# Chunked scan of a hybrid block: cumulative steps made once and broadcast by DMA, decays formed on ScalarE, two products moved to GpSimd

## The reference

```
xdt = x * dt[..., None]
a_cum = jnp.cumsum(dt * a.reshape(G, R), axis=2)
seg = a_cum[:, :, :, None] - a_cum[:, :, None]
decay_ls = jnp.exp(jnp.where(causal, seg, -jnp.inf))
cb = jnp.einsum("bclgn,bcsgn->bclsg", cm, bm)
y_diag = jnp.einsum("bclsg,bclsgr,bcsgrp->bclgrp", cb, decay_ls, xdt)
decay_to_end = jnp.exp(a_cum[:, :, -1:] - a_cum)
states = jnp.einsum("bclgn,bclgr,bclgrp->bcgrpn", bm, decay_to_end, xdt)
...  # h <- h * exp(a_cum[-1]) + states, from chunk to chunk
y_off = jnp.einsum("bclgn,bcgrpn,bclgr->bclgrp", cm, h_start, jnp.exp(a_cum))
y = y_diag + y_off + x * d_skip.astype(f32).reshape(G, R)[:, :, None]
```

## Time and profile before

| | us |
|---|---|
| median of three runs | 2776.07 |
| profiled execution | 2777.77 |
| its span | 2776.1 |
| TensorE busy (matmul) | 2617.1 |
| VectorE busy | 1783.4 |
| GpSimd busy | 1590.2 |
| ScalarE busy | 1307.3 |

### The profile page before, as it was taken

How to read it: one execution, slowest core, us unless ns; L and a number is a source line. 1 busy time by engine, 2 the same in 40 slices (tenths; PEclk the granted TensorE clock), 3 DMA queues, 4 the chain that set the end, 5 groups by cost and what they waited for, 6 DMA issues and landing times. The chain is left out here.

```text
span 2776.1 us, 41535 instructions
## 1 busy us (share of the span) xinstructions
PE 2617.1 (94%) x14314; PEld 1845.0 (66%) x14314; DVE 1783.4 (64%) x2181; ACT 1307.3 (47%) x2067; POOL 1590.2 (57%) x1222
## 2 busy tenths in 40 slices
PE   4799999997999999899989999999999999599998
PEld 3588777776888888666655555555555555478887
DVE  4632356536313545189979888898988989555554
ACT  2433333344333333211148787877877778422221
POOL 3777666678777777468746666566655666000000
PEclk8799999998999999999989999999999999799999
DMA  2343333332433333335551212212122111333231
GB/s 103 99 145 135 105 120 106 125 102 89 160 118 109 127 133 118 102 82 134 131 169 33 86 61 62 77 39 85 62 62 68 48 39 58 112 127 106 76 107 44
DMA packets 202405, 267.97 MB, mean 97 GB/s; under 512 B 12832, under 2 KB 136032, under 8 KB 195568
## 3 DMA queue, kind: packets, MB, share of 16 engines
q1 hardware_dynamic: 202224, 265.64, 30.1%
HBM read 168.84 MB, written 96.76 MB: 96 GB/s over the span
## 5 line engine op out<-in xcount | busy, mean ns | idle before, releaser
L1935 POOL TENSOR_TENSOR a_w<-a_beta,a_rest 128x1024 f32<-128x1024 f32 (+2 forms) x320 | 560.8, 1753 | 354.6 <-DVE a_rest L1892 208.1
L808 POOL TENSOR_TENSOR f_l_lo<-f_wst,f_l_hi 128x512 fp32r<-128x512 f32 x312 | 407.2, 1308 | 273.6 <-ACT f_l_hi L702 272.6
L1892 DVE TENSOR_TENSOR_SCAN a_rest<-a_keep,a_rest,a_ones 128x513 f32<-128x513 f32 x384 | 469.9, 1261 | 10.8 <-ACT a_keep L1862 10.8
L1812 PE MATMUL a_turn<-a_ident,a_w 128*128 128x128 f32 (+1 forms) x2432 | 343.7, 279 | 7.3 <-DVE a_wt L1846 6.1
L1827 PE MATMUL a_o<-a_wt,a_v 128*64 128x512 f32 (+3 forms) x1408 | 339.6, 561 | 8.9 <-DVE a_out L1902 8.9
L1846 ACT COPY a_wt<-a_turn 128x512 f32<-128x512 f32 (+3 forms) x440 | 225.3, 528 | 208.0 <-PE a_turn L1812 206.5
L1812 PEld LDWEIGHTS a_turn<-a_ident,a_w 128*128 128x128 f32 (+1 forms) x2432 | 257.4, 140 | 91.5 <-issue 65.4
L1862 ACT ACTIVATE a_keep<-a_z 128x1024 f32<-128x1024 f32 (+4 forms) x352 | 299.8, 852 | 4.5 <-PE a_z L1795 4.5
L702 ACT ACTIVATE f_l_hi<-f_wst 128x512 fp32r<-128x512 f32 x312 | 195.7, 628 | 222.2 <-PE f_y L605 106.6
L1862 ACT ACTIVATE a_beta<-a_z 128x1024 f32<-128x1024 f32 (+4 forms) x352 | 299.6, 851 | 0.0
L605 PE MATMUL f_y<-f_t_hi,f_l_hi 128*128 128x512 f32 x624 | 249.9, 401 | 14.8 <-DVE f_u L1093 9.3
(11 more groups left out here) (228 smaller groups left out, 4988.6 us busy)
## 6 DMA issues: line engine op xcount, KB each, us to landing
f_wst<-in_w_pairs SPq DMA_DIRECT2D x52, 1024.0 KB, 5.4
scratch_gate<-f_out SPq DMA_DIRECT2D x64, 256.0 KB, 2.2
o_g<-scratch_mixed SPq DMA_DIRECT2D x32, 512.0 KB, 5.6
s_xc<-scratch_xbc SPq DMA_DIRECT2D x16, 768.0 KB, 5.2
scratch_xbc<-f_out SPq DMA_DIRECT2D x36, 256.0 KB, 2.1
scratch_q_hi<-f_out SPq DMA_DIRECT2D x32, 256.0 KB, 3.3
scratch_q_lo<-f_out SPq DMA_DIRECT2D x32, 256.0 KB, 3.6
scratch_v<-f_out SPq DMA_DIRECT2D x32, 256.0 KB, 2.3
```

Source lines behind the costliest of these rows:

```text
L808: return nc.gpsimd.tensor_tensor(out, a, b, op).then_inc(done, 1)
L1812: mm = nc.tensor.transpose(turn[h][0:rows, qi * P:(qi + 1) * P], tile[:, h, x:x + rows], ident[:, :])
L1892: mm = nc.vector.tensor_tensor_scan(rest[r % RS][:, h, tn - 1::-1], top, ones[:, 0:1].to_broadcast([P, tn]), start, ALU.mult, ALU.min)
L1935: nc.gpsimd.tensor_tensor(w[r % AS][:, :, 0:tn], beta[r % KEEPS][:, :, 0:tn], rest[r % RS][:, :, 1:tn + 1], ALU.mult).then_inc(w_ready, 1)
```

## The change

scan_start now makes, for all 16 chunks at once, the running sums of the steps in two layouts. One has the tokens on partitions: three products of 256 columns (psums), whose exp is kept as `scan.sums` (running sum, sum to the end, total), and whose first part is kept as it is in `scan.total`. The other has (chunk, head) on partitions and goes to a new scratch tensor `cum`. From there each unit loads its 8 rows of 128 sums, broadcast over all 128 partitions (`load_cum`, 512 KB, one buffer per s and g), issued by SP ahead of the store of group 0.

In scan_stage the products s_pc and s_pseg on TensorE, s_ua on GpSimd and s_expo on ScalarE are gone. ScalarE forms each decay as exp(-relu(own sum - loaded sum)): eight Relu of 128x128 with the token's own sum as bias, then a wait for them, then one Exp over 1024 columns in place. GpSimd takes over s_xde (`to_end`) and the state's fade (`fade`); its list becomes to_end(+1), fade(0), skip(+1), gate(-1). VectorE's state sum waits for the fade.

```
@@ -1164,6 +1164,10 @@
+        self.sums = self.sbuf("s_sums", [P, 3, NT, HEADS])
+        self.total = self.sbuf("s_total", [P, NT, HEADS])
+        self.cum = [[self.sbuf(f"s_cum{s}{g}", [P, HPG, P]) for g in range(GROUPS)] for s in range(2)]
+        self.cum_loaded = [self.sems(f"s_cum_loaded{s}", GROUPS) for s in range(2)]
@@ -1174,6 +1178,10 @@
                      .rearrange("b p t -> p b t")).then_inc(self.zt_loaded[s], 16)
+    def load_cum(self, sp, s, g, i):
+        sp.dma_start(self.cum[s][g][:, :, :], self.scratch["cum"][bass.ds(i * 2 + s, 1), g * HPG:(g + 1) * HPG, :]
+                     .to_broadcast([P, HPG, P])).then_inc(self.cum_loaded[s][g], 16)
@@ -1222,10 +1236,19 @@
                          .rearrange("b p t -> p b t")).then_inc(loaded, 16)
+            sp.wait_ge(cum_ready, START + 2)
+            for b in range(2):
+                sp.dma_start(scratch["cum"][b * (NT // 2):(b + 1) * (NT // 2), :, :].rearrange("t h l -> (t h) l"),
+                             by_step[b][:, :]).then_inc(cum_stored, 16)
             scan.loads(sp)
+            sp.wait_ge(cum_stored, START + 32)
+            for s in range(2):
+                for g in range(GROUPS):
+                    scan.load_cum(sp, s, g, 0)
         def _(pool):
+            scan.constants(pool)
             nc.gpsimd.memset(ident[:, :], 0.0).then_inc(made, 1)
@@ -1233,11 +1256,21 @@
                                     pattern=[[-1, META]], channel_multiplier=1).then_inc(ready, 1)
-            scan.constants(pool)
             attention.constants(pool)
         def _(pe):
+            pe.wait_ge(scan.made, 4)
+            pe.wait_ge(steps_ready, START + 1)
+            for b in range(2):
+                last = nc.tensor.matmul(ps[:, 0, b * P:(b + 1) * P],
+                                        steps[:, b * (NT // 2):(b + 1) * (NT // 2), :].rearrange("p t h -> p (t h)"),
+                                        scan.upper[:, :], start=True, stop=True)
+            last.then_inc(cum_done, 1)
+            for q, lhs in enumerate((scan.upper, scan.later, scan.ones)):
+                last = nc.tensor.matmul(psums[:, q, :], lhs[:, :], steps[:, :, :].rearrange("p t h -> p (t h)"),
+                                        start=True, stop=True)
+            last.then_inc(sums_done, 1)
             pe.wait_ge(ready, START + 2)
@@ -1253,12 +1286,20 @@
         def _(act):
+            act.wait_ge(cum_done, START + 1)
+            for b in range(2):
+                nc.scalar.copy(by_step[b][:, :], ps[:, 0, b * P:(b + 1) * P]).then_inc(cum_ready, 1)
+            act.wait_ge(sums_done, START + 1)
+            nc.scalar.activation(scan.total[:, :, :].rearrange("p t h -> p (t h)"), psums[:, 0, :], ACT.Copy).then_inc(sums_ready, 1)
+            nc.scalar.activation(scan.sums[:, :, :, :].rearrange("p q t h -> p q (t h)"), psums[:, 0:3, :],
+                                 ACT.Exp).then_inc(sums_ready, 1)
             act.wait_ge(turned, START + 1)
         def _(dve):
+            nc.vector.tensor_copy(steps[:, :, :], dt_tok[:, 1:NT + 1, 1, :]).then_inc(steps_ready, 1)
             dve.wait_ge(turned, START + 1)
@@ -1358,6 +1409,10 @@
                 for s in range(2):
+                    if more:
+                        for g in range(GROUPS):
+                            sp.wait_ge(decay_ready[s][g], i + 1 + START)
+                            scan.load_cum(sp, s, g, i + 1)
                     store(s, 0, i)
@@ -1379,11 +1434,20 @@
-            def spread_steps(s, g, i):
-
-                pool.wait_ge(seg_ready[1 - s][g], i + s + START)
-                nc.gpsimd.tensor_tensor(ua[g][:, :, :], upper[:, :].unsqueeze(1).to_broadcast([P, HPG, P]),
-                                        over_heads(dt_of(i, s, 1, g), P), ALU.mult).then_inc(ua_ready[s][g], 1)
+            def to_end(s, g, i):
+                hs = slice(g * HPG, (g + 1) * HPG)
+                pool.wait_ge(xdt_ready[s][g], i + 1 + START)
+                pool.wait_ge(st_done[1 - s][g], i + s + START)
+                nc.gpsimd.tensor_tensor(heads(xde[g]), heads(xdt[g]), over_heads(sums_of(i, s, 1, hs), HEAD),
+                                        ALU.mult).then_inc(xde_ready[s][g], 1)
+            def fade(s, g, i):
+                hs = slice(g * HPG, (g + 1) * HPG)
+                pool.wait_ge(off_done[s][g], i + 1 + START)
+                own = state[:, g, :].rearrange("p (h c) -> p h c", h=HPG)
+                nc.gpsimd.tensor_tensor(own, own, over_heads(sums_of(i, s, 2, hs), HEAD), ALU.mult).then_inc(decayed[s][g], 1)
@@ -1398,7 +1462,7 @@
-            pipeline(pool, (2, spread_steps), (1, skip), (-1, gate))
+            pipeline(pool, (1, to_end), (0, fade), (1, skip), (-1, gate))
@@ -1415,23 +1479,11 @@
                     last.then_inc(bc_ready[s], 1)
-                    pe.wait_ge(expo_ready[1 - s], i + s + START)
-                    for n, lhs in enumerate((upper, later, ones)):
-                        rhs = (dt_tok[:, 1 + 2 * i + s, 1, :] if isinstance(i, int) else
-                               dt_tok[:, bass.ds(i * 2 + (1 + s), 1), 1, :].rearrange("p o h -> p (o h)"))
-                        last = nc.tensor.matmul(pc[:, n, :], lhs[:, :], rhs, start=True, stop=True)
-                    last.then_inc(sums_ready[s], 1)
                 ps, pg, count = before(s, g, i)
                 last.then_inc(x_turned[s][g], 1)
-                pe.wait_ge(ua_ready[s][g], i + 1 + START)
-                pe.wait_ge(decay_ready[ps][pg], count + START)
-                for half in range(2):
-                    hs = slice(half * (HPG // 2), (half + 1) * (HPG // 2))
-                    last = nc.tensor.matmul(pseg[:, hs, :], later[:, :], ua[g][:, hs, :], start=True, stop=True)
-                last.then_inc(seg_ready[s][g], 1)
@@ -1465,12 +1517,14 @@
                     nc.scalar.activation(b_tok[s][:, :, :], pbc[:, 0:GROUPS, :], ACT.Copy).then_inc(b_ready[s], 1)
-                    act.wait_ge(sums_ready[s], i + 1 + START)
-                    act.wait_ge(decayed[s][1], i + START)
-                    nc.scalar.activation(expo[s][:, :, :], pc[:, :, :], ACT.Exp).then_inc(expo_ready[s], 1)
-                act.wait_ge(seg_ready[s][g], i + 1 + START)
+                act.wait_ge(scan.cum_loaded[s][g], i * 16 + 16 + START)
                 act.wait_ge(m_ready[1 - s][g], i + s + START)
-                nc.scalar.activation(decay[g][:, :, :], pseg[:, :, :], ACT.Exp).then_inc(decay_ready[s][g], 1)
+                for h in range(HPG):
+                    last = nc.scalar.activation(decay[g][:, h, :], scan.cum[s][g][:, h, :], ACT.Relu,
+                                                bias=total_of(i, s, g * HPG + h), scale=-1.0)
+                last.then_inc(span_ready[s][g], 1)
+                act.wait_ge(span_ready[s][g], i + 1 + START)
+                nc.scalar.activation(decay[g][:, :, :], decay[g][:, :, :], ACT.Exp, scale=-1.0).then_inc(decay_ready[s][g], 1)
@@ -1492,13 +1542,9 @@
                 dve.wait_ge(diag_done[1 - s][g], i + s + START)
+                dve.wait_ge(xde_ready[1 - s][g], i + s + START)
                 nc.vector.tensor_tensor(heads(xdt[g]), px[:, :, :].rearrange("p b (h c) -> p (b h) c", h=2),
                                         over_heads(dt_of(i, s, 0, g), HEAD), ALU.mult).then_inc(xdt_ready[s][g], 1)
-                dve.wait_ge(xdt_ready[s][g], i + 1 + START)
-                dve.wait_ge(expo_ready[s], i + 1 + START)
-                dve.wait_ge(st_done[1 - s][g], i + s + START)
-                nc.vector.tensor_tensor(heads(xde[g]), heads(xdt[g]), over_heads(expo[s][:, 1, hs], HEAD),
-                                        ALU.mult).then_inc(xde_ready[s][g], 1)
@@ -1511,10 +1557,8 @@
                 dve.wait_ge(off_done[s][g], i + 1 + START)
-                nc.vector.tensor_tensor(heads(yo[g]), heads(pyo), over_heads(expo[s][:, 0, hs], HEAD),
+                nc.vector.tensor_tensor(heads(yo[g]), heads(pyo), over_heads(sums_of(i, s, 0, hs), HEAD),
                                         ALU.mult).then_inc(yo_ready[s][g], 1)
-                own = state[:, g, :].rearrange("p (h c) -> p h c", h=HPG)
-                nc.vector.tensor_tensor(own, own, over_heads(expo[s][:, 2, hs], HEAD), ALU.mult).then_inc(decayed[s][g], 1)
                 dve.wait_ge(decayed[s][g], i + 1 + START)
@@ -2206,7 +2250,7 @@
     shapes = {"k_hi": [PAIRS, P, T], "k_lo": [PAIRS, P, T], "q_hi": [PAIRS, P, SEQ], "q_lo": [PAIRS, P, SEQ],
-              "xbc": [XB, P, T], "gate": [MB, P, SEQ], "v": [T, D], "mixed": [MB, P, SEQ]}
+              "cum": [NT, HEADS, P], "xbc": [XB, P, T], "gate": [MB, P, SEQ], "v": [T, D], "mixed": [MB, P, SEQ]}
     scratch = {name: nc.dram_tensor(f"scratch_{name}", shape, F32, kind="Internal").ap() for name, shape in shapes.items()}
...
```

More of the change, by code:

```diff
@@ L1213, in scan_start @@
         ps = m.psum("s0_ps", [P, GROUPS, W])
+        psums = m.psum("s0_psums", [P, 3, NT * HEADS])
+        steps = m.sbuf("s0_steps", [P, NT, HEADS])
```

(26 more changed lines are left out.)

## The result

The changed kernel takes 2786.8 us (2780.72 to 2790.02), the kernel before 2777.0 on the same chip: a ratio of 1.0036, interval 1.0025 to 1.0048. That is slower by more than the 0.2% that can be told from no change. The forecast was 2779.3, of no difference that could be told; the time lies in its range of 2761 to 2797, above the likeliest case's own 2771 to 2786. Of the three outcomes the prediction had given slower the largest chance, 0.38.

What follows compares the result with a forecast made beforehand. Bound: the loop from GpSimd's gate through SP to the next s_xc load, 14.30 us a chunk against 13.82. +6.2 over 13 periods and -3 for start and tail gave 2781.0 profiled, 2779.3 median; range 2761 to 2797.

Steps and rivals of the forecast that it cites:

- likeliest case: Scan: the input load's loop holds at about the old period; 2771 to 2786 by itself, chance 0.42.
- The loop through GpSimd's gate, SP and the load: Scan chunk: gate end, 0.78 to the s_xc issue, 5.17 to the next s_pbc; 13.72 us before clock and scatter.
- t of the gate's end, 7.77 warm: GpSimd: gate ends 7.77 us after s_pbc starts, at full clock, behind to_end, fade, skip and s_mt; 7.69 before.
- Rival 1: GpSimd: the gate comes before s_mt, gate end 6.77, chunk 12.72, -16 us, 2760; chance 0.22.
- The low clock, 0.4 a chunk: TensorE: half clock after the load wait delays fade; 0.4 us a chunk taken, bounds 0 and 1.7.
- rival 3: TensorE: low clock holds for the whole front, chunk 15.4 + 0.18, +20 us, 2796; chance 0.26.
- The sum of the steady part: Scan loop: 14.12 us a chunk plus 0.18 scatter, 14.30 against 13.82; +6.2 us over 13 periods.
- Start and tail, -3: Scan's ends: first s_xc issue about 2 us earlier net, next stage's loads some 0.9 earlier; -3, bounds -6 and +2.
- ScalarE 3.3 a unit, hidden: ScalarE: eight Relu and one Exp take 3.3 us a unit, decay ready before s_mt asks for it.
- The new loads, 0: SP's queue: two 512 KB loads per chunk fit idle DMA time, cost 0; up to 1 us a chunk if colliding.
- Rival 2: Scan: the load's loop does not bind, the turn-to-turn chain decides, 11.7 us a chunk, -30 us, 2746; chance 0.10.
- Profiled execution to median: Whole kernel: median of the timed runs lies 1.7 us under the profiled execution, so 2781.0 becomes 2779.3.

Runs made afterwards that it cites:

- SP's order: Changed kernel with SP issuing the s_xc load, then the two loads of sums, ahead of both stores: 2743.12 us, ratio 0.9885, the fastest kernel.
- the last two orders: Changed kernel with SP's order alone, 2743.12 us, and with GpSimd's gate also ahead of skip, 2759.13 us.

## Why the prediction was nearly right

- *The loop through GpSimd's gate, SP and the load holds the chunk at about the old period or above.* Right: 14 waits for s_xc of 14, and 27 us come back when SP no longer waits for the gate first.
- *t of the gate's end, 7.77 warm.* 7.90 measured. to_end and fade take 1.04 each, as taken from s_xd. s_mt comes before the gate in order, and the margin was just about the 0.33 named: it starts at 1272.98 and the gate's record at 1273.30. Rival 1's order was 0.3 us away, and two chunks of the run with one eighth of the sums had it. Its price of 2760 was not tested by the 2759.8 of the run with the gate ahead of skip: there the gate ended at 6.08 instead of rival 1's 6.77, and s_pbc came 6.17 behind the issue instead of 5.17, so the agreement is luck.
- The Trainium skill says that the two engines exclude each other, an operation of VectorE with two SBUF inputs and one of GpSimd that reads SBUF (SBUF — State Buffer, Who interferes with whom). The trace agrees: 1.27 or 2.25 for the same gate, by who asks first.
- *The low clock, 0.4 a chunk.* This is the term that was mis-sized. It fell in 11 of 14 chunks, which is rival 3's condition, but for 0.83 in most of them instead of the 1.7 priced, since only the front up to a part of s_pyo ran at half clock; one chunk lost 1.5. The mean is 0.65 (8.53 - 7.88). Reality lies between forecast and rival 3.
- *The sum of the steady part.* Forecast 14.30, measured 14.74: 0.25 from the clock, 0.1 from the gate, 0.1 from issue and scatter. 13 x 0.44 = 5.7 us, which makes up the 5.8 between +3.2 and the +9.0 of the scan.
- *Start and tail, -3.* Measured -3.1, split otherwise: the first loop issue came 38.08 after the scan's first load instead of 39.18 (-1.1 where -2 was taken), the tail gave -2.0 instead of -0.9. The first s_pbc stands 18.95 behind the scan's first load (1163.72 to 1182.67), 16.97 before: +2.0 for the products ahead where 2.6 was priced (by the 3.62 of the earlier trace rows it would be 2.7). So the first chunks without s_ua and s_pseg returned 3.1 and not the 4.6 that the -2 rests on. That the two errors cancel to -3.1 is luck.
- *ScalarE 3.3 a unit, hidden.* 3.5 (2.43 + 1.06), still hidden: s_decay is there at 1272.37, 0.6 before s_mt starts.
- *The new loads, 0.* Right, by the run with one eighth of them; they landed in 6.0 in the middle, as the broadcast of the earlier trace rows did.
- *Rival 2, a load that doesn't bind.* False for this kernel. Its chain is the next bound all the same: priced at 11.7 a chunk and 2746, it took 11.56 and 2743.12 once SP's order freed the load.
- *Profiled execution to median.* Taken as 1.7 above the median; it was 6.1 below, as it fell on the shortest run. That it took 2780.72 where 2781.0 was forecast is luck: the stages ahead were 5.0 shorter and the scan 5.8 longer than forecast.

What stays open is what shares the clock and the gate's place have in the 16 us between the last two orders, why waits of one length lowered the clock in some chunks and not in others, and why s_xc lands after 5.0 to 6.3 within one kernel.

## What to carry to other kernels

When three chains have nearly one length, work taken from two of them is worth nothing, and what counts is where its operations land in the third: here ahead of the instruction for which SP, and through it the next load, waits. Follow a load back to what issues it, and put loads on the queue ahead of stores that wait for a late operation; then the same change gives 1.15% instead of costing 0.36%. A wait that opens on TensorE can be paid twice, as the products after it may run at half clock, and an instrument that hides that must fit in the gap.

## What the runs showed of the hardware

- TensorE lost its clock around waits of only 2.3 to 3.5 us a chunk, in 11 of 14 chunks: 0.90 granted in the stretch, products of 0.60 in 1.06, and 1.00 with filler in the gaps.
- Eight Relu of 128x128 on ScalarE with a bias column took 2.43, 0.388 each by the group's mean in the trace, and follow each other every 0.29:

```profile
L1523 ACT ACTIVATE s_decay<-s_cum,s_total 128x128 f32<-128x128 f32 x248 | 75.5, 388 | 0.0
```

- The recorded length of one of these products on GpSimd or VectorE includes its wait for the other: the gate had 1.27, 1.72 and 2.25 us (ahead of skip, before, after the change), for the same work. The shortest of a tile's durations is its own time, the rest is who came first:

```profile
L1552 DVE TENSOR_TENSOR s_mt<-s_decay,s_cbm x31: 1245/1440/1444, 1192.6 to 1410.3; 128x1024 f32<-128x1024 f32 x31
```

- In the loop ScalarE goes from Copy to Relu to Exp with no table load between them, and the Exp takes 1.06 (at 1271.31) where it took 1.025 before. At the scan's start one table load of 1.28 stands ahead of the first Exp:

```profile
1169.53 1.28 ACT L1294 ACT_TABLE_LOAD   x1
```

- DMA engines were busy 0.85 of the time in the fastest kernel, and its input load still came in time; issued 7.5 us or more ahead, it could land after 6.4 at no cost:

```profile
1207.00:1380.00 173.00, 144.89 (x897) 108.05 (x895) 139.09 (x189) 100.47 (x266) 148.23 (x114) 0.98 0.85 251
```
